# Key norms of a recurrence summed per head in 16 partitions, in one stage with the first unit's preparation

## The reference, cut to what matters

```
kkr = heads(k * p['k_k'])
kk  = kkr / jnp.maximum(jnp.sqrt(jnp.sum(kkr * kkr, axis=-1, keepdims=True)), 1e-12)
decay = exp(-exp(-softplus(-(w0 + tanh(w1d) @ w2)) - 0.5))
a  = sigmoid(a1d @ a2 + a0);   kd = k * (1 + (a - 1) * k_a)
S  = S * decay - (S @ kk) * (kk * a) + v * kd       # per token
```

## Time and profile before

| | |
|---|---|
| median of three runs | 6409.04 us |
| profiled execution, span from its first to its last instruction | 6443.3 us |
| busy: PE, PEld, DVE, ACT, POOL | 53%, 44%, 58%, 16%, 29% |
| key norm and operands of unit one, first call | 559.26 to 602.64 us |
| second, third and fourth call | 1545.71, 2791.72 and 4037.42 us to 1589.03, 2834.54 and 4080.83 us |

### The profile page before, as it was taken

One profiled execution on the slowest core, in us unless ns is written; L12 is line 12 of the kernel. 1 busy time (PEld: TensorE's weight loads), 2 busy tenths in 40 slices (PEclk: granted clock), 3 DMA queues, 4 the chain that ended last, 5 costly groups with the idle time before them and its releaser, 6 DMA issues. The chain is left out here.

```text
span 6443.3 us, 89825 instructions
## 1 busy us (share of the span) xinstructions
PE 3410.4 (53%) x33664; PEld 2825.2 (44%) x33664; DVE 3735.1 (58%) x6968; ACT 1010.8 (16%) x2406; POOL 1859.8 (29%) x1550
## 2 busy tenths in 40 slices
PE   8867877377676304266620078688400000644988
PEld 1556766266565303155520067576300000543777
DVE  0255561756887684778878823564478888243110
ACT  0112331011332000023310011341100000111110
POOL 0000000132553572125567700000058877000000
PEclk9878999688777657577755589899755555865999
DMA  8322003265774895257789943001169999300332
GB/s 314 114 77 73 3 9 111 100 256 186 238 236 151 293 357 194 71 176 237 240 279 356 351 129 117 12 3 57 61 234 335 340 357 356 128 3 15 122 123 114
DMA packets 295558, 1116.70 MB, mean 173 GB/s; under 512 B 33312, under 2 KB 38704, under 8 KB 289968
## 3 DMA queue, kind: packets, MB, share of 16 engines
q0 software_dynamic: 221184, 805.40, 35.6%
q1 hardware_dynamic: 74032, 306.49, 14.3%
HBM read 1110.72 MB, written 1.05 MB: 173 GB/s over the span
## 5 line engine op out<-in xcount | busy, mean ns | idle before, releaser
L153 PE MATMUL psum<-h,weight_ring 128*128 128x256 f32 x5440 | 1223.1, 389 | 145.5 <-PEq L79 134.1
L153 PEld LDWEIGHTS psum<-h,weight_ring 128*128 128x128 f32 x5440 | 1062.8, 196 | 305.8 <-issue 137.3
L1344 POOL DMA_INDIRECT ring<-in_peer_u,expert x496 | 611.2, 1232 | 1541.6 <-SPq L79 741.9
L1561 DVE SCALAR_TENSOR_TENSOR tok<-ring,act,tok 128x1024 f32<-128x1024 f32 x688 | 883.9, 1285 | 117.6 <-DMA ring<-in_peer_v,expert_group 81.7
L1513 POOL DMA_INDIRECT ring<-in_peer_v,expert_group x688 | 797.6, 1159 | 223.8 <-issue 212.6
L1597 PE MATMUL psum<-constants,tok 128*128 128x128 f32 x48 | 10.6, 414 | 1589.1 <-PEq L79 1589.1
L1597 PEld LDWEIGHTS psum<-constants,tok 128*128 128x128 f32 x48 | 9.7, 225 | 1589.9 <-issue 1589.9
L1324 DVE CUSTOM_DVE_ANT_0 ring<-ring,tok 128x1024 f32<-128x1024 f32 x496 | 597.4, 1222 | 172.5 <-DMA ring<-in_peer_u,expert 157.3
L1513 POOL DMA_INDIRECT ring<-in_peer_u,expert_group x272 | 345.8, 1271 | 735.5 <-DVE expert_group L1549 657.2
L1556 DVE CUSTOM_DVE_ANT_0 ring<-ring,tok 128x1024 f32<-128x1024 f32 x272 | 330.6, 1227 | 89.8 <-DMA ring<-in_peer_u,expert_group 86.9
L153 PE MATMUL psum<-m,weight_ring 128*128 128x256 f32 x768 | 177.7, 396 | 54.9 <-PEq L79 54.9
(11 more groups left out here) (501 smaller groups left out, 6363.0 us busy)
## 6 DMA issues: line engine op xcount, KB each, us to landing
weight_ring<-in_w_in SPq DMA_DIRECT2D x228, 512.0 KB
ada_ring<-in_ada_w SPq DMA_DIRECT2D x24, 2048.0 KB
weight_ring<-in_w_q SPq DMA_DIRECT2D x48, 512.0 KB
weight_ring<-in_w_out SPq DMA_DIRECT2D x32, 512.0 KB
weight_ring<-in_w_gate SPq DMA_DIRECT2D x32, 512.0 KB
weight_ring<-in_w_mlp_in SPq DMA_DIRECT2D x32, 512.0 KB
weight_ring<-in_w_mlp_out SPq DMA_DIRECT2D x8, 2048.0 KB
weight_ring<-in_w_oB SPq DMA_DIRECT2D x24, 512.0 KB
```

Source lines behind the costliest of these rows:

```text
L153: mm = pe.matmul(k.bank(slot, tokens), ring[:, slot, j * P:j * P + P], rhs(j), start=(j == 0), stop=(j == w.kt - 1))
L1344: pool.indirect_dma_start(job.ring[:, r % HOSTED, :], None, job.tables[kind], bass.IndirectOffsetOnAxis(ap=job.eidx[:, number:number + 1], ...
L1561: dve.scalar_tensor_tensor(job.tok[:, tile, :], r.ring[:, j, :], r.act8[:, part, j:j + 1], job.tok[:, tile, :], ALU.mult, ALU.add).then_in ...
```

## The change

The key norm's stage and the part for the first unit are taken out, and a function `key_norms` stands in their place. It is one stage. Squares are taken from `z` itself, with `k_k` as the activation's scale, one activation for each of eight blocks. TensorE computes the low-rank products, then adds the eight blocks' squares into one 16 by 256 sum (bank 4), one partition for each head. Root, maximum and reciprocal work on these 16 by 256 numbers, and eight products by `head_spread` carry the result to 128 partitions (banks 4 to 7). VectorE multiplies `kk` by it in two halves. `squares` uses the memory of `G`, `norm` that of `TT`. GpSimd's part is written first, so `fetch_rows` sees `job.row` as the stage before left it. Two constants are new in the first table; six masks move to the second, two are dropped.

```diff
+def key_norms(k, L, b, first, emit):
+    squares = b.G[:]...("p (j t) -> p j t", j=8); norm = b.TT[0:16]...[:, 0:256]
+    with k.stage() as block:
+        @block.gpsimd
+        def _(pool):
+            pool.memset(b.W[:], 0.0).then_inc(k.pool_step.up(), 1)
+            fetch_rows(k, pool)
+        @block.tensor
+        def _(pe):
+            pe.wait_ge(k.act_step.sem, k.act_step.at(1))
+            first.low_rank(pe)
+            for j in range(8):
+                pe.wait_ge(k.act_step.sem, k.act_step.at(1 + j + 1))
+                mm = pe.matmul(k.bank(4, 256)[0:16, :], k.head_rows[:, 14 - 2 * j:30 - 2 * j], squares[:, j, :], start=(j == 0), stop=(j == 7))
+            mm.then_inc(k.multiplied.up(), 1)
+            pe.wait_ge(k.vec_step.sem, k.vec_step.at(INVERTED))
+            for j in range(8):
+                mm = pe.matmul(k.psum[:, 2048 + 256 * j:2304 + 256 * j], k.head_spread[0:16, P * j:P * j + P], norm, start=True, stop=True)
+                if j % 4 == 3:
+                    mm.then_inc(k.multiplied.up(), 1)
+        @block.scalar
+        def _(act):
+            act.activation(z[:, 24, :], z[:, 24, :], ACT.Tanh).then_inc(k.act_step.up(), 1)
+            for j in range(8):
+                act.activation(squares[:, j, :], kz[:, j, :], ACT.Square, scale=L.k_k[:, j:j + 1]).then_inc(k.act_step.up(), 1)
+            if emit:
+                act.activation(z[:, 26:28, :], z[:, 26:28, :], ACT.Sigmoid)
+            first.sigmoids(act)
+            act.wait_ge(k.multiplied.sem, k.multiplied.at(1))
+            act.activation(norm, k.bank(4, 256)[0:16, :], ACT.Sqrt).then_inc(k.act_step.up(), 1)
+        @block.vector
+        def _(dve):
+            chain(dve.tensor_tensor(kk[:], kz, over_tokens(L.k_k, 8, 256), ALU.mult))
+            dve.wait_ge(k.act_step.sem, k.act_step.at(11))
+            chain(dve.tensor_scalar(norm, norm, 1e-12, None, ALU.max))
+            chain(dve.reciprocal(norm, norm))
+            use_rows(k, dve, 1)
+            first.sums(dve)
+            for n in range(2):
+                dve.wait_ge(k.multiplied.sem, k.multiplied.at(2 + n))
+                chain(dve.tensor_tensor(part, part, k.psum[:, 2048 + 1024 * n:3072 + 1024 * n]..., ALU.mult))
+            use_rows(k, dve, 2)
+        block.scalar(first.exponentials)
+        block.vector(first.rates)
+        block.vector(first.scaled)
...
 def rwkv_unit(k, b, operands, following):
-        if operands.first:
-            ... (memset of W, low_rank, sigmoids, sums, exponentials, rates, scaled)
...
 constants, first table:
-        "up", "lo", "up_incl", "lo_incl", "up8", "lo8", "up_far", "lo_far"
+        "head_rows": p // 64 == np.arange(30)[None, :] - 14,
+        "head_spread": p == 2 * (column // P) + column % P // 64,   # 1024 columns
 second table:
+        "lo", "up_incl", "lo_incl", "up8", "lo8", "up_far"
```

More of the change, by code:

```diff
@@ L745, in _ @@
             if operands.first:
-                act.wait_ge(k.pool_step.sem, marks["cleared"])
+                act.wait_ge(k.pool_step.sem, k.pool_step.count)
             if sweep == 0:
@@ L1002, in buffers @@
     return names(**{name: mem.enter_context(k.sbuf(name, shape)) for name, shape in shapes.items()})
+def key_norms(k, L, b, first, emit):
+    z, kk = b.z, b.kk
+    kz = z[:, 8:16, :]
+    squares = b.G[:].rearrange("p h i n t -> p (h i n t)").rearrange("p (j t) -> p j t", j=8)
+    norm = b.TT[0:16].rearrange("p i n t -> p (i n t)")[:, 0:256]
+    with k.stage() as block:
[28 more added lines that the diff above has]
+        def _(dve):
+            chain = chained(k, dve)
+            chain(dve.tensor_tensor(kk[:], kz, over_tokens(L.k_k, 8, 256), ALU.mult))
[6 more added lines that the diff above has]
+                dve.wait_ge(k.multiplied.sem, k.multiplied.at(2 + n))
+                part = kk[:, 4 * n:4 * n + 4, :]
+                chain(dve.tensor_tensor(part, part, k.psum[:, 2048 + 1024 * n:3072 + 1024 * n].rearrange("p (j t) -> p j t", j=4), ALU.mult))
+            use_rows(k, dve, 2)
+        block.scalar(first.exponentials)
+        block.vector(first.rates)
+        block.vector(first.scaled)
@@ L1005, in rwkv @@
+INVERTED = 3
 def rwkv(k, L, z, states, emit, o=None, spare=None):
@@ L1011, in rwkv @@
         b = buffers(k, mem, kk=[8, 256])
[L1013 to L1037, removed]
-                act.wait_ge(k.multiplied.sem, k.multiplied.at(1))
-                act.activation(s.norm[:], k.psum[:, 0:2048].rearrange("p (j t) -> p j t", j=8), ACT.Sqrt).then_inc(k.act_step.up(), 1)
-            @block.tensor
-            def _(pe):
-                pe.wait_ge(k.act_step.sem, k.act_step.at(1))
-                for j in range(8):
-                    mm = pe.matmul(k.psum[:, 256 * j:256 * j + 256], k.blocks64, s.squares[:, j, :], start=True, stop=True)
-                mm.then_inc(k.multiplied.up(), 1)
         if emit:
```

14 lines of the change are left out of this document (8 added, 6 removed).

## The result

The changed kernel took 6322.95 us (median of 4 runs, 6319.46 to 6346.78) beside 6409.46 for the kernel before (4 runs, 6403.09 to 6420.76): ratio 0.9868, 95% interval 0.9849 to 0.9886, or 86.5 us less. It was run twice more, on two chips: 0.9866 [0.9829, 0.9904] and 0.9888 [0.9874, 0.9903]. The three ratios, in this order, are 84.6, 85.9 and 71.8 us of 6409. The forecast was 62.9 us with an end of its range at 77. The direction and the chain were right, the time was too high.

A forecast was written before the change was run, and what follows sets the result against it. Bound: a relay with one runner in the key norm's stage, VectorE's 2048-column reciprocal included. Gains of 17.9, 17.9, 14.9 and 13.2 us over four calls, less 1.0 for constants, make 62.9: 6409.0 to 6346 us, range 6332 to 6363.

The forecast's parts named there:

- from there on the unit runs as before: Behind the start of the transposes of `C` (L805) nothing changes, so time taken from the chain is taken from the kernel.
- the warm rival: TensorE's clock stays high through both sets of products; L796 to L817 warm it up to 1 us earlier; gain 72, 6337; 17%.
- the middle taken for the spreading: First and fourth call: gain 19.4 or 16.5 us by TensorE's clock while spreading the norms; 17.9 taken for each.
- The reciprocal: In the norm stage on VectorE: 1.75 us for 16 partitions by 256 columns instead of 12.95 for 2048 columns.
- ScalarE and TensorE level at the root, t = 7.7: In the norm stage, ScalarE's table load and TensorE's products both end 7.7 us after VectorE's product by `k_k` starts.
- Low-rank products within 1 us of the stage's start: Sign to look for: TensorE starts the low-rank products from 0.6 us into the norm stage, within 1 us of its start.
- Second and third call: Calls with expert rows now in the open: gain 14.9 us in the second, 13.2 in the third with its exposed table load.
- its cover: In the unit's stage, the second gathered row is used by 5.6 us, before VectorE's masks, with 0.4 us to spare.
- The expert rows' rival: Gathers never catch up, so each of 496 rows waits longer; at 0.2 us more a row, 6445 and slower; 3%.
- The constants: The second constant table grows from 640 to 1024 KB in an exposed load, 3.8 to 4.8 us, a loss of 1.0.
- The table rule: The skill page adds a 1.38 us drain to a table switch: root 1.4 us later each call, sum 57, not 63.
- Profiled time against the median: The profiled 6443.3 us lies 34.3 above the plain median; the same microseconds come off both, giving 6380 and 6346.

The follow-up runs named there:

- the chain paid back: The changed kernel with reciprocals of spare data added on VectorE, so each call's chain is about as long as before the change; ratio 0.997 to the kernel before.
- the late values alone: The kernel before with one added wait, so TensorE turns the first unit's values right ahead of the transposes of `C`; ratio 0.9998 to the kernel before.

## Why the prediction was wrong

The step that failed is the end of the first paragraph, "from there on the unit runs as before", and with it the size in the warm rival: L796 to L817 "without a gap" would "warm TensorE up to 1 us earlier". The term stood at nothing in the sum. The clock rose 2.0 to 2.6 us earlier in the changed kernel (3.4 in the kernel before with its values turned late), and, with the later falls that changed too, the units were 5 us a call shorter. This step explains a part of the excess only; the larger part stays open, as the sums below show. With the values turned right ahead of `C` the two units' stretches took 643.6 to 647.5 us in seven profiles, with the old gap or the values a stage ahead 654.7 to 659.0 in four. The changed kernel's three profiles average 646.8 against 656.1 for the two of the kernel before: 9.3 us that the sum held at nothing. I had priced the mechanism by the distance between two instructions and not by a row of the clock behind them, though the trace of before had it: 0.50 for 6 us behind L805.

So 65.2 (chain and load) and 9.3 make 74.5. The three measurements are 71.8, 84.6 and 85.9, with intervals of 62 to 81, 73 to 97 and 62 to 110 us; 74.5 lies inside all three. But of the 9.3 us only 4.6 are left at the next pass over the experts (1010.6 us on average against 1015.2), and the kernel's end behind the last pass is 2.7 us longer, the load taken off (944.1 against 940.5). Every stretch that repeats, added up, gives 67 us. The 5 to 19 us above that in the three measurements lie in stretches that scatter between two profiles of the same kernel, in calls two and three and in the passes over the experts, and no run here finds them. Runs that change little or nothing of the chain don't settle it either: the chain paid back kept 19 us (10 to 29), the late values alone kept 1 (-5 to 8).

The forecast's 63.9 us of chain against 66.1 measured was nearly right, and mostly not by luck: its steps came true one by one, and only the middle taken for the spreading was chance. Its total was too small by 22 us in the first measurement (84.6), of which 2 are chain and load and 5 to 9 the clock in the units; 10 to 17 are open.

Point by point, by the prediction's own steps:

- The reciprocal: 1.74 us four times, 1.75 said. The maximum 0.28, 0.3 said. Right.
- ScalarE and TensorE level at the root, t = 7.7: the root started at t = 7.43, both releases within 0.1 us. Squares 0.41 apart, 0.40 said. Right. In the third call TensorE came last by 0.63 us, and the root 2.8 us later than in the first, 0.9 to 2.5 said.
- Low-rank products within 1 us of the stage's start: 0.43. Right.
- The spreading at high clock or low: in between. The clock was 1.00 at 571 and 0.50 at 573; the second product of VectorE waited 1.25 us. So the middle between the two cases came true, 24.95 where 25.45 was said; that the clock would fall halfway the prediction didn't know, and this much is luck.
- Second and third call: 16.2 and 13.5 us gained, 14.9 and 13.2 said. The first wait for a row in the unit's stage was 2.37 us, under 3, and the masks followed it at once, 4.13 us behind L790, so its cover held.
- The expert rows' rival: the DMA wait over 496 rows was 178.7, 179.1 and 188.7 us in the changed kernel's profiles, 157.3 and 174.6 in those of the kernel before. Some growth may be there; two profiles of one kernel are 17 us apart, so it isn't shown, and the whole didn't get longer by it.
- The constants: 3.8 to 4.7 us, 4.8 said.
- The table rule: the root started 0.01 us behind the end of its load, with no drain of 1.38. The Trainium skill (page "ScalarE: Activation LUTs", section "What ACT_TABLE_LOAD costs") states some 1.38 us of drain on top of the load. Worked out from it, as an estimate, the root would start at 569.1. The trace disagrees with the drain, on either side of the load (the last sigmoid ended at 566.46, the load started at 566.48), and agrees with the load's 1.28.
- Profiled time against the median: the same microseconds were to come off both. The spans of the changed kernel were 6318.3, 6352.8 and 6354.8, those of the kernel before 6443.3 and 6381.2. A single pair would have given anything between 26 and 125 us. It was right to sum a chain and not to subtract spans.

The range failed with the sum: its low end was the warm case with all its chain terms at high clock, and the case with the chain in the middle and the unit warm had no place in it.

## What to carry to other kernels

Where a change moves work of TensorE, look at what its clock does behind the stage that you count, over the whole stretch to the next fixed point, and price that stretch from its own rows; "from there on as before" is a term of the sum like any other. Small hidden work placed right ahead of a long stretch of matrix products may be worth more there than its own length, and moving it out of the way can cost what it saves. Then look whether the gain is still there one stretch further on: here half of it was gone. Reductions per head belong in as few columns as possible before an operation whose time goes by columns, and the order inside the stage is worth another look after it: 16 us of chain were left here, about half in VectorE's order and half in the place of the values.

## What the runs showed of the hardware

- The reciprocal's time goes by columns alone: 1741 ns for 16 partitions by 256 columns, 1753 for 128 by 256, 12953 for 2048 columns, 5.08 us for 788.
- The clock's rises and falls repeat for the most part in the calls without expert rows. Counted from the product by `k_k`, the changed kernel's first call had them at 1.9, 5.3, 12.1, 29.2, 97.4 and 100.9 us in all three profiles, within 0.1 us, on two chips at least. Later falls can differ: two of the three have one more, 243 us behind `C`, and the kernel before's first call was low at 81 to 92 us behind `C` in one profile and at 75 to 78 in the other.
- The later the clock rose behind `C`, the sooner it fell again. Over calls one and four of all fourteen profiles: risen after 5.4 to 6.3 us, the first fall came after 33 us; after 4.6 to 4.7, at 39 or 80; after 3.9 to 4.3, at 72 to 79; after 3.6 to 3.8, at 161; after 2.7 to 2.9, at 160 to 235. Ahead of the kernel before's fall at 33.5 TensorE was busy for 2.33 of 3.41 us. Why the falls stand where they do isn't shown.
